# A dense-layer weight slot keeps its low part in place of the raw weights, and the ring of high parts grows from two slots to four

## What is computed

```python
for i in range(DEPTH):
    if i % N_MIXERS == 0:
        mix, h, c = _rglru_mixer(x, lru_h[j], lru_conv[j], ...)
    else:
        mix, s, c = _gdn_mixer(x, gdn_s[j], gdn_conv[j], ...)
    x = _layer_norm(DN_ALPHA * x + mix, p['ln_g'][i, 0], p['ln_b'][i, 0])
    xa = _mem_attention(x, mem_k[i], mem_v[i], p['xa_wq'][i], p['xa_wo'][i])
    x = _layer_norm(DN_ALPHA * x + xa, p['ln_g'][i, 1], p['ln_b'][i, 1])
    if i % 2 == 0:
        ff = _swiglu(x, p['ffn_w_gu'][j], p['ffn_w_down'][j], D_FF)
    else:
        ff = _moe_ffn(x, p['moe_router'][j], p['moe_w_gu'][j], p['moe_w_down'][j])
    x = _layer_norm(DN_ALPHA * x + ff, p['ln_g'][i, 2], p['ln_b'][i, 2])
```

## Time and profile before

| what | value |
| --- | --- |
| median of three runs | 2546.24 us |
| lowest and highest run | 2544.56 and 2550.89 us |
| span of the profiled execution | 2548.9 us |
| busy: PE, PEld | 2310.6 us (91%), 2190.4 us (86%) |
| busy: DVE, ACT, POOL | 905.0 us (36%), 541.8 us (21%), 988.9 us (39%) |
| moved by DMA | 348.08 MB, mean 137 GB/s |

### The profile page before, as it was taken

How to read it: one execution, slowest core, us unless ns; L and a number is a source line. 1 busy time by engine, 2 the same in 40 slices (tenths; PEclk the granted TensorE clock), 3 DMA queues, 4 the chain that set the end, 5 groups by cost and what they waited for, 6 DMA issues and landing times.

```text
span 2548.9 us, 42792 instructions
## 1 busy us (share of the span) xinstructions
PE 2310.6 (91%) x17174; PEld 2190.4 (86%) x17174; DVE 905.0 (36%) x1485; ACT 541.8 (21%) x1022; POOL 988.9 (39%) x1397
## 2 busy tenths in 40 slices
PE   8998889899999997999999788878599999999993
PEld 8988867899999987888888678848599999999993
DVE  3674423411011158777777545224101000000004
ACT  2351321310011033333333221232100000111103
POOL 4647535588888947333333007705200000000001
PEclk9999999899999999999999889999699999999996
DMA  7314442222222222122122112440456577788884
GB/s 290 99 59 160 157 158 91 91 84 89 92 83 86 87 91 69 52 62 62 62 62 62 37 44 98 182 182 17 178 182 204 193 249 242 241 257 281 280 288 159
DMA packets 98649, 348.08 MB, mean 137 GB/s; under 512 B 13504, under 2 KB 18752, under 8 KB 93616
## 3 DMA queue, kind: packets, MB, share of 16 engines
q1 hardware_dynamic: 73136, 279.08, 32.6%
q10 hardware_dynamic: 19328, 45.18, 5.2%
q0 software_dynamic: 6016, 21.43, 2.3%
HBM read 319.19 MB, written 26.47 MB: 136 GB/s over the span
## 4 chain that ended last, share of the span: by engine, by line
PE 63%; issue 14%; DVE 9%; POOL 6%; DMA 4%; ACT 3%; ACTq 0%; POOLq 0%; DVEq 0%; SPq 0%
PE ps L554 26%; PE ps L1144 14%; PE ps L1159 8%; PE ps L794 4%; POOL wl L476 3%; DMA raw<-weights 3%; POOL wh L472 2%; PE ps L655 1%; DVE x L1770 1%; PE ps L1005 1%; PE ps L1001 1%; PE ps L984 1%; PE ps L659 1%; PE ps L841 1%; DVE x L1758 1%
## 5 line engine op out<-in xcount | busy, mean ns | idle before, releaser
L472 POOL TENSOR_TENSOR wh<-raw,tab 128x256 fp32r<-128x256 f32 x672 | 439.7, 685 | 806.3 <-PE ps L554 541.2
L476 POOL TENSOR_TENSOR wl<-raw,wh 128x256 fp32r<-128x256 f32 x672 | 521.1, 806 | 0.0
L1144 PE MATMUL ps<-work,raw 128*128 128x128 f32 (+6 forms) x3072 | 424.3, 299 | 13.0 <-DMA raw<-weights 10.6
L1144 PEld LDWEIGHTS ps<-work,raw 128*128 128x128 f32 x3072 | 419.6, 191 | 16.3 <-issue 9.4
L554 PE MATMUL ps<-xh,wh 128*128 128x272 f32 x2048 | 306.1, 300 | 49.0 <-POOL wl L476 17.0
L554 PEld LDWEIGHTS ps<-xh,wh 128*128 128x128 f32 x2048 | 276.7, 195 | 63.6 <-issue 26.1
L554 PE MATMUL ps<-xh,wl 128*128 128x272 f32 x2048 | 297.5, 295 | 0.0
L554 PE MATMUL ps<-xl,wh 128*128 128x272 f32 x2048 | 280.9, 289 | 0.0
L554 PEld LDWEIGHTS ps<-xh,wl 128*128 128x128 f32 x2048 | 275.8, 194 | 1.8 <-issue 0.5
L554 PEld LDWEIGHTS ps<-xl,wh 128*128 128x128 f32 x2048 | 266.1, 189 | 0.0
L523 POOL DMA_DIRECT2D rows_y<-moe_h x8 | 4.3, 540 | 656.9 <-DVE moe_h L2255 656.9
(11 more groups left out here) (378 smaller groups left out, 2987.3 us busy)
## 6 DMA issues: line engine op xcount, KB each, us to landing
raw<-weights SPq DMA_DIRECT2D x488, 512.0 KB, 4.1
moe_h<-cache SPq DMA_DIRECT2D x6, 2048.0 KB, 9.2
moe_h<-cache ACTq DMA_DIRECT2D x4, 2048.0 KB, 15.3
work<-cache SPq DMA_DIRECT2D x4, 2048.0 KB, 8.7
moe_h<-rows_x POOLq DMA_DIRECT2D x14, 512.0 KB, 8.0
rows_x<-lnsq ACTq DMA_DIRECT2D x9, 512.0 KB, 10.9
work<-scratch ACTq DMA_DIRECT2D x16, 272.0 KB, 4.2
work<-cache ACTq DMA_DIRECT2D x2, 2048.0 KB, 10.5
```

Of the source, the lines that this page charges most:

```text
L472: nc.gpsimd.tensor_tensor(flat(h1[:, k0:k1]), flat(r1[:, k0:k1]), one_col, MUL).then_inc(pool_hi, 1)
L476: low = nc.gpsimd.tensor_tensor(flat(l1[:, k0:k1]), flat(r1[:, k0:k1]), flat(h1[:, k0:k1]).bitcast(F), SUB)
L1144: last = mm(ps[:, j // 2, (j % 2) * c:(j % 2 + 1) * c], raw[:, slot % RAW, k, :], M_x[:, r % 2, k, 0:c], start=(k == 0), stop=(k == KT - 1))
```

## The change

The low part is written over the raw slot: `wl` becomes a second name of `raw`'s memory with the type fp32r, four slots long, and `wh` has four slots in the memory that `wh` and `wl` had. So raw slot j holds the raw weights, then the low part, until PE is done. Every load of SP now waits for `w_used` of the slot four back, POOL's wait for `w_used` is gone (the landing implies it), and PE takes slot s from place s mod 4. Since a half of the SwiGLU's output product takes 6 slots, the place depends on the half, so `down` is written out twice where it was a loop of two.

```diff
-RAW, SPLIT, PIECES = 4, 2, 4
+RAW, PIECES = 4, 4
...
-        wh = sb("wh", [P, SPLIT, KT, P], R)
-        wl = sb("wl", [P, SPLIT, KT, P], R)
+        wl = nc.alloc_sbuf_tensor_at("wl", [P, RAW, KT, P], R, offset=nc.sbuf_base - 4 * RAW * KT * P)
+        wh = sb("wh", [P, RAW, KT, P], R)
...
-            def load(t, offset, shift, lo=0, hi=RAW):
+            def load(t, shift):
...
-                for j in range(lo, hi):
-                    if offset is None:
-                        ge(sp, w_used, t * RAW + (j + 1 - RAW))
-                    else:
-                        ge(sp, w_split, t * RAW + (j + 1 - RAW - offset))
+                for j in range(RAW):
+                    ge(sp, w_used, t * RAW + (j + 1 - RAW))
...
                     pool.wait_ge(w_in[j], t * 16 + 16)
-
-                    ge(pool, w_used, t * RAW + (j + 1 - SPLIT - (first if j < SPLIT else 0)))
-                    h1, l1, r1 = wh[:, j % SPLIT], wl[:, j % SPLIT], raw[:, j]
+                    h1, l1, r1 = wh[:, j], wl[:, j], raw[:, j]
...
-                    lin_tile(slot + s, direct, s % 2, s % 2, ah, al)
+                    lin_tile(slot + s, direct, s % RAW, s % 2, ah, al)
...
-                            lin_tile(e36 + g * 4 + j, direct, j % 2, j, xh, xl)
+                            lin_tile(e36 + g * 4 + j, direct, j, j, xh, xl)
...
-                                    last = mm(ps[:, 2 * d + h, 0:HT], w[:, s % 2, k, :], a[:, f, h * HT:(h + 1) * HT],
+                                    last = mm(ps[:, 2 * d + h, 0:HT], w[:, (2 * g + s) % RAW, k, :], a[:, f, h * HT:(h + 1) * HT],
...
-                    if isinstance(e, int) and e + e0 == 0:
-                        down(0)
-                        down(1)
-                    else:
-                        with pe.Fori(0, 2) as g:
-                            down(g)
+                    down(0)
+                    down(1)
...
-                    yield from lin_steps(S_GDN + 4 * h + j, 28, j % 2, 0, xh, xl, per=per, fresh=None if j else fresh)
+                    yield from lin_steps(S_GDN + 4 * h + j, 28, j, 0, xh, xl, per=per, fresh=None if j else fresh)
...
-                    lin_tile(S_LRU[b] + 2 + j, 8 + 4 * (b // 2), j, j, xh, xl)
+                    lin_tile(S_LRU[b] + 2 + j, 8 + 4 * (b // 2), 2 + j, j, xh, xl)
```

More of the change, by code:

```diff
@@ L393, in _, with turns @@
         def _(sp):
-            def load(t, offset, shift, lo=0, hi=RAW):
-                for j in range(lo, hi):
-                    if offset is None:
-                        ge(sp, w_used, t * RAW + (j + 1 - RAW))
-                    else:
-                        ge(sp, w_split, t * RAW + (j + 1 - RAW - offset))
+            def load(t, shift):
+                for j in range(RAW):
+                    ge(sp, w_used, t * RAW + (j + 1 - RAW))
                     sp.dma_start(raw[:, j:j + 1, :, :], I["weights"][ds(t * RAW + (j + shift), 1)].rearrange(
                         "o p (k c) -> p o k c", k=KT)).then_inc(w_in[j], 16)
-            def turns(slot, n, before, own, dram):
+            def turns(slot, n, dram):
                 t0 = slot // RAW
-                load(t0, before, dram - slot)
+                load(t0, dram - slot)
                 if n > RAW:
                     with sp.Fori(t0 + 1, t0 + n // RAW) as t:
-                        load(t, own, dram - slot)
+                        load(t, dram - slot)
             def cache(l):
@@ L417, in cache @@
                         c_in[i % RING], 16)
-            load(0, None, W_KV0)
+            load(0, W_KV0)
             sp.wait_ge(w_in[0], 16)
             sp.dma_start(x[:, :, :], I["xT"]).then_inc(ld_x, 16)
[L423 to L430, removed]
+            turns(S_KV0[1], RAW, W_KV0 + 4)
+            turns(S_LRU[0], 2 * RAW, W_LRU)
+            turns(S_KV0[2], RAW, W_KV0 + 8)
+            turns(S_LRU[2], RAW, W_LRU + 8)
+            turns(S_LRU[3], RAW, W_LRU + 12)
+            turns(S_KV0[3], RAW, W_KV0 + 12)
+            turns(S_LOUT, 8, W_LOUT)
+            turns(S_KV1[0], 4, W_KV1)
             for l in range(NL):
-                d = (20, 32)[l]
-                turns(S_Q[l], 8, None, d, W_Q0 if l == 0 else W_Q1)
-                turns(S_O[l], RAW, d, d, (W_Q0 if l == 0 else W_Q1) + 8)
+                turns(S_Q[l], 8, W_Q0 if l == 0 else W_Q1)
+                turns(S_O[l], RAW, (W_Q0 if l == 0 else W_Q1) + 8)
                 cache(l)
-                turns(S_O[l] + RAW, RAW, d, d, (W_Q0 if l == 0 else W_Q1) + 8 + RAW)
+                turns(S_O[l] + RAW, RAW, (W_Q0 if l == 0 else W_Q1) + 8 + RAW)
                 if l == 0:
[L438 to L442, removed]
+                    turns(S_KV1[1], 4, W_KV1 + 4)
+                    turns(S_FFN, HALVES * 36, W_FFN)
+                    turns(S_KV1[2], 4, W_KV1 + 8)
+                    turns(S_GDN, 4 * GH + 8, W_GDN)
+                    turns(S_KV1[3], 4, W_KV1 + 12)
             sp.wait_ge(r_dve, ORDER)
@@ L461, in _, with split @@
             one_col = tc("ones", 0, 1).to_broadcast((P, KT * P // PIECES))
-            def split(t, first, offset):
+            def split(t, offset):
                 for j in range(RAW):
                     pool.wait_ge(w_in[j], t * 16 + 16)
-                    ge(pool, w_used, t * RAW + (j + 1 - SPLIT - (first if j < SPLIT else 0)))
-                    h1, l1, r1 = wh[:, j % SPLIT], wl[:, j % SPLIT], raw[:, j]
+                    h1, l1, r1 = wh[:, j], wl[:, j], raw[:, j]
                     for q in range(PIECES):
@@ L477, in split, with turns @@
                     low.then_inc(w_split, 1)
-            def turns(slot, n, first, offset):
+            def turns(slot, n, offset):
                 t0 = slot // RAW
-                split(t0, first, offset)
+                split(t0, offset)
                 if n > RAW:
                     with pool.Fori(t0 + 1, t0 + n // RAW) as t:
[L484 to L491, removed]
+                        split(t, offset)
+            turns(S_LRU[0], 2 * RAW, 8)
+            turns(S_LRU[2], 2 * RAW, 12)
+            turns(S_LOUT, 8, 16)
+            turns(S_Q[0], 16, 20)
+            turns(S_FFN, HALVES * 36, 24)
+            turns(S_GDN, 4 * GH + 8, 28)
+            turns(S_Q[1], S_MOE - S_Q[1], 32)
             pool.wait_ge(r_dve, COUNTED)
@@ L495, in _ @@
             with pool.If(over > 0):
-                turns(S_MOE, NE * 36, 0, 32)
+                turns(S_MOE, NE * 36, 32)
             with pool.Else():
```

## The result

The changed kernel took 2580.93 us in the median of four runs (2577.82 to 2587.11), before 2548.56 in the same comparison (2544.56 to 2551.18): a ratio of 1.0122, with a 95% interval of 1.0100 to 1.0144. It is slower by some 32 us; forecast were 2527.3, and 2511 to 2541 as the range. The profiled executions have spans of 2577.6 and 2548.9 us, 28.7 apart.

A forecast was written before the change was run, and what follows sets the result against it. PE carried 63% of the chain that ended last, with POOL's splits part of the bound. Terms 27.0 + 6.4 - 13.0 - 1.5 = 18.9 us, taken off 2546.2, gave 2527.3 us; range 2511 to 2541.

The forecast's parts named there:

- the splits move against DVE: Delta-rule heads and four LayerNorms: splits beside DVE slow its operations, costing 13.0 + 1.5 us; far end 0.69 us an operation.
- The gain of 33.4 us: Openings and short waits: PE's waits for POOL (27.0 us) and the slow clock after stalls (6.4 us) go.
- 302.7 to 309.4: First queries' opening: when the fifth slot is ready, against PE's need at 308.2; covered except the worst landing (1.2 us).
- Costs of 0 for the loads, the in-place pass and the written-out loop: Loads waiting for PE, low part over the raw slot, and `down` written out twice: each taken to cost 0.
- The rival of the slower low pass: POOL's splits: in-place low pass at twice its time makes POOL the bound, 2632 us; chance 0.04.
- 35 x 0.37 = 13.0 us: Delta rule, heads 0 to 5: six DVE operations a head (head 0 lacks one), each 0.37 us longer beside splits.
- the longer idle in each head drops PE's clock: Delta rule, heads 0 to 5: one drop a head costs 7.8 us more, 2535.1; two drops, 2542.9; chance 0.13.
- As a far end, one piece of POOL's low pass: DVE beside splits: the most an operation would sit out, 0.69 us; at that price 6.5 us gained, 2539.7 us.
- The rival on the other side: POOL's splits: the in-place low pass is slower and POOL becomes the bound, 2632 us; chance 0.04.

The follow-up runs named there:

- the last combination: Changed kernel with POOL waiting for its own last low pass before each split, and a three-slot lead in the delta rule's turn: 2515.50 us, ratio 0.9854.
- the lead of two: Changed kernel, but POOL again waits everywhere until PE has used all but the last slot, as before: 2551.83 us, ratio 1.0004.
- the lead in the heads: Changed kernel with POOL at most three slots ahead of PE's releases, not four, in the delta rule's turn alone: 2542.98 us, ratio 0.9983.
- the break: Changed kernel, lead still four, but POOL waits for the end of its own last low pass before the next split: 2555.82 us, ratio 1.0033.

## Why the prediction was wrong, point by point

Forecast was 18.9 us less; measured are some 32 us more. The step that failed is the price of "the splits move against DVE": 13.0 + 1.5 us in the sum, with 0.69 us an operation as the most that it could be, and nothing for PE's clock. In its place the runs showed DVE operations shut out for up to 16.47 us by POOL's unbroken runs, and in the heads a longer idle of PE that drops the clock. An estimate from the rows: 33.4 won, less 40.4 in the heads, 10.2 up to the RG-LRU's output and 13.3 in the two waits of L668, makes 30.5 us lost; the two profiled executions are 28.7 apart.

- **The gain of 33.4 us held.** The waits went from 27.0 to 1.2 us, and the third slots of the openings run at the full clock. (The fifth slot's "302.7 to 309.4" adds up to 302.6 to 309.3; nothing hangs on it.) With the two losses taken away, the last combination is 0.9835 to 0.9873 of before, 32 to 42 us less; 33.4 lies within, though that kernel still waits 3.1 us for POOL.
- **Costs of 0 for the loads, the in-place pass and the written-out loop were right** as costs of their own, shown together by the lead of two at 1.0004; with the lead of four, the load that must land first is what moves the splits in the heads. The rival of the slower low pass fell: four pieces take 2.8 us alone, before and after.
- **"35 x 0.37 = 13.0 us" for DVE in the heads** had the places and the price right, and two operations too few. Forecast was 1.1 us more idle at each place. Measured are 2.13 - 0.64 = 1.49 and 2.06 - 0.80 = 1.26, and DVE accounts for both: before L991, the four operations from L2007 to L2051 went from 0.69, 0.18, 0.73 and 0.79 to 0.97, 0.59, 1.19 and 1.13 us, together 1.49; before L1015 another four gained 1.28. The mean is 0.35 an operation. I had counted three at each place and left out L2051 and L1738 (L2061 and L1748 before).
- **The rival "the longer idle in each head drops PE's clock" is what happened in the heads; its price failed.** I gave it 0.13 and 1.3 us a drop, from the shortest stall in the earlier trace rows. From PE's second wait to the product of the next step (L921) head 1 takes 1165.37 - 1144.90 = 20.47 us, before 1158.36 - 1143.61 = 14.75: 5.7 us. With the idle that makes 1.5 + 1.3 + 5.7 = 8.5 us a head against 8.3 measured. Evidence against it was a single wait, 1.82 us at 143.50 without a drop; that two such waits follow each other within one head was in the chain that I had read; I priced one drop and two drops a head, each at 1.3 us, and did not weigh the two waits together.
- **"As a far end, one piece of POOL's low pass" (0.69 us) is where the price failed outright.** I took it for a bound; it was the longest delay that short runs of POOL can show. Before, POOL waited for PE 541.2 us in 110 waits, and these waits, which I counted only as lost lead, were also the breaks that let DVE in. Taken away, one operation paid 16.47 us. The Trainium skill ("SBUF — State Buffer", Who interferes with whom) says that the one that issues first has the shared ports for the whole instruction while the other blocks. The traces agree that it is a block and not a slowing, for a `TENSOR_SCALAR`, a `COPY` and a `TENSOR_TENSOR` with two SBUF inputs; they differ in length, for L1896 sat out 25 further POOL instructions and not the rest of one. Where I let POOL run ahead at no cost, in the RG-LRU and up to the scores, DVE's next operation came into that run.
- **The rival on the other side** was sought in the wrong place: I asked what would make POOL slower. POOL was as fast as forecast; it was too steady.

The losses in the table are undone by the two remedies: in the last combination PE starts on the RG-LRU's output at 204.27, heads 0 to 6 take 378.0 us (before 377.9) and the second attention 63.1 (before 63.8). Against the changed kernel's ratio of 1.0122 the lead in the heads is worth 1.4%, the break 0.9%, both 2.7%. That is 0.4% over the sum of the two; the intervals, some 0.2% on each of the four ratios, just allow this to be nothing. So no third cost shows, but a small interplay of the two is not excluded.

## What to carry to other kernels

A wait that one engine makes for another can do two jobs: it limits the lead, and it spaces the engine's work. Before removing it, look for what runs in its gaps, above all DVE operations on SBUF beside a long GpSimd stream; where the stream may run on, put a wait on its own last instruction every 8 pieces (runs of 16 showed no shut-out either, in a single run). And when a load becomes the releaser in place of PE's release, everything behind it moves by the load's latency: keep one slot more loaded than may be worked on, so that the release still starts the work.

## What the runs showed of the hardware that I had not expected

- A DVE operation without a PSUM operand that came when GpSimd had begun 17 or more instructions in a row, with no such DVE operation among them, waited in all 30 cases until the run ended: 16.47 us for an operation that takes 0.58 alone. A break of 0.14 us in the run lets it in.
- A DVE that works along from the start of POOL's run, or keeps working inside a long one, is not shut out: from 139.03 on in the changed kernel two splits ran beside DVE, stretched by some 0.3 us a piece, and eight operations of L1738 in a row at the 20th to 27th piece of a run of 32 (from 291.73) took 0.86 to 1.15 us each.
- Two waits of PE of some 2 us each, some 20 us apart, were followed by 13.7 us at the lower clock in 17 of 20 heads; one of them alone mostly by 3.4 us of it or by nothing, and by 13.7 us in 1 of 10.
